# Selected and recent scores of the last attention as three products of rounded parts

## What is computed

```python
def nsa_attention(q, kc, vc, ks, vs, kw, vw, gate_logits, ...):
    qh = q.reshape(B_, S, NSA_KV, NSA_HPG, NSA_DH)... * (NSA_DH ** -0.5)
    ...
        sc = jnp.einsum('bghqd,bgjd->bghqj', qb, kcmp) + head_bias(rel_c)
        ...
        ss = jnp.einsum('bghqd,bgqkd->bghqk', qb, kg) + bias_s
        ps = masked_softmax(ss, (rel_s >= 0)[:, :, None])
        osel = jnp.einsum('bghqk,bgqkd->bghqd', ps, vg)
        ...
        sw = jnp.einsum('bghqd,bgkd->bghqk', qb, kwb) + head_bias(rel_w)
        pw = masked_softmax(sw, mask_w)
        ow = jnp.einsum('bghqk,bgkd->bghqd', pw, vwb)
        return gb[:, 0, ..., None] * oc + gb[:, 1, ..., None] * osel + gb[:, 2, ..., None] * ow
```

## Time and profile before

| | |
|---|---|
| median of 3 runs | 3185.5 us (3185.4 to 3188.45) |
| the profiled execution | 3188.14 us, its span 3186.6 us |
| busy: PE, PEld, DVE, ACT, POOL | 3063.3, 2472.8, 1313.5, 1186.2, 1105.1 us |
| granted TensorE clock, mean | 0.989 |
| the last attention, scores of the third unit to the end of the quarters | 2786.29 to 2996.00 us of the span |
| L1542 (all scores of this function) | 352 MATMUL records, 2177.7 to 2991.3 us |
| who waited for L1542 | DVE L1589, 119.1 us in 122 waits |

### The profile page before, as it was taken

The page is one execution under the profiler, slowest core; times in us unless marked ns, Lnnn a source line. Parts: engine busy times, 40 slices in busy tenths (PEclk is TensorE's granted clock), DMA queues, the critical chain, the costliest instruction groups (busy, mean ns, idle before and its releaser), DMA issues.

```text
span 3186.6 us, 36178 instructions
## 1 busy us (share of the span) xinstructions
PE 3063.3 (96%) x14292; PEld 2472.8 (78%) x14292; DVE 1313.5 (41%) x2362; ACT 1186.2 (37%) x2090; POOL 1105.1 (35%) x463
## 2 busy tenths in 40 slices
PE   8999998899999999999989999989999999999998
PEld 6888777678888878887858888877768878866787
DVE  5311386723111451112874231285544252256532
ACT  3222375743232442223424332353333342355432
POOL 4444432024444444444004444433424423300143
PEclk9999999999999999999999999999999999999999
DMA  4333232013333223333213333323313325400032
GB/s 146 93 99 97 83 123 69 1 47 99 99 93 99 93 86 99 98 95 100 89 40 113 99 99 93 99 89 104 100 53 99 93 89 179 132 2 1 28 98 73
DMA packets 78188, 278.27 MB, mean 87 GB/s; under 512 B 8600, under 2 KB 9496, under 8 KB 77637
## 3 DMA queue, kind: packets, MB, share of 16 engines
q1 hardware_dynamic: 78020, 275.96, 27.5%
HBM read 273.78 MB, written 6.08 MB: 88 GB/s over the span
## 4 chain that ended last, share of the span: by engine, by line
PE 84%; DVE 10%; ACT 3%; issue 2%; POOL 1%; DMA 0%; ACTq 0%; SPq 0%; DVEq 0%; POOLq 0%
PE ps L486 24%; PE ps L488 24%; PE ps L487 24%; PE ps L1568 3%; PE ps L1542 2%; DVE arena L2440 1%; DVE arena L1824 1%; PE ps L1554 1%; PE ps L3135 1%; PE ps L2490 1%; DVE w_lo L471 1%; PE ps L1988 1%; PE ps L2931 1%; PE ps L1974 1%; POOL w_lo L461 1%
## 5 line engine op out<-in xcount | busy, mean ns | idle before, releaser
L461 POOL TENSOR_TENSOR w_lo<-ring,w_hi 128x1024 fp32r<-128x1024 f32 x447 | 1090.5, 2441 | 1949.4 <-ACT w_hi L438 1908.0
L486 PE MATMUL ps<-x_hi,w_hi 128*128 128x512 f32 x2168 | 858.0, 396 | 35.0 <-POOL w_lo L461 21.9
L488 PE MATMUL ps<-x_hi,w_lo 128*128 128x512 f32 x2168 | 847.6, 391 | 0.0
L487 PE MATMUL ps<-x_lo,w_hi 128*128 128x512 f32 x2168 | 847.2, 391 | 0.0
L438 ACT CAST w_hi<-ring 128x1024 fp32r<-128x1024 f32 x473 | 493.9, 1046 | 723.9 <-PE ps L488 714.6
L486 PEld LDWEIGHTS ps<-x_hi,w_hi 128*128 128x128 f32 x2168 | 409.5, 189 | 127.9 <-issue 19.6
L487 PEld LDWEIGHTS ps<-x_lo,w_hi 128*128 128x128 f32 x2168 | 409.6, 189 | 88.2 <-issue 4.1
L488 PEld LDWEIGHTS ps<-x_hi,w_lo 128*128 128x128 f32 x2168 | 409.0, 189 | 86.2
L486 PE MATMUL ps<-r_hi,w_hi 128*128 128x512 f32 x1120 | 436.3, 390 | 0.0
L487 PE MATMUL ps<-r_lo,w_hi 128*128 128x512 f32 x1120 | 435.7, 389 | 0.0
L488 PE MATMUL ps<-r_hi,w_lo 128*128 128x512 f32 x1120 | 435.7, 389 | 0.0
(11 more groups left out here) (269 smaller groups left out, 3320.7 us busy)
## 6 DMA issues: line engine op xcount, KB each, us to landing
ring<-in_stream SPq DMA_DIRECT2D x473, 512.0 KB, 3.5
arena<-in_cmp_w SPq DMA_DIRECT2D x16, 512.0 KB, 3.8
frev_copies<-frev SPq DMA_DIRECT2D x16, 240.0 KB
arena<-frev_copies SPq DMA_DIRECT2D x1, 3072.0 KB, 13.1
h<-in_x SPq DMA_DIRECT2D x4, 512.0 KB, 8.0
out<-arena SPq DMA_DIRECT2D x4, 512.0 KB
arena<-in_p SPq DMA_DIRECT2D x2, 512.0 KB
arena<-in_mem SPq DMA_DIRECT2D x1, 1024.0 KB
```

The lines of the kernel that those rows point to most:

```text
L461: self.nc.gpsimd.tensor_tensor(self.w_lo[:, n % SPLIT, :], self.ring[:, n % RING, :], self.w_hi[:, n % SPLIT, :].bitcast(F32), ALU.subtrac ...
L486: nc.tensor.matmul(out, a[0], b[0], start=start, stop=False)
L487: nc.tensor.matmul(out, a[0], b[1], start=False, stop=False)
L488: return nc.tensor.matmul(out, a[1], b[0], start=False, stop=stop)
```

## The change

The scores of the selected and recent units (not of the compressed ones) are computed by `product` from high and low parts, of keys and of queries. The parts of the keys are made once in `compress_and_project`: ACT's evacuation of the last 4 groups writes float32r into `mem_hi`, and DVE, after its 64 small preparations, subtracts that from PSUM into `mem_lo` (4 of 128x512). The arrays of the memory operand serve as room for the keys' parts. The parts of a query are made in `attention`, once per group, two groups ahead: ACT rounds it to `r_hi` (`round`), DVE subtracts (`rest`) into `r_lo`; there are 8 places of 128 columns. ACT's rounding stands before the exponentials of a group's first unit, DVE's subtraction before the bias of a group's last unit. PE waits for the group's subtraction ahead of s and w. ACT also waits at the start for the values and for the keys' low parts.

```diff
-        self.w = key.shape[-1]
+        self.w = (key[0] if isinstance(key, tuple) else key).shape[-1]
+class Queries:
+    PLACES = 8
+    AHEAD = 2
+    def __init__(self, k, q, scored):
+        s = k.s
+        self.k, self.q, self.scored = k, q, scored
+        self.hi, self.lo = (x[:, :, :].rearrange("p a b -> p (a b)") for x in (k.r_hi, k.r_lo))
+        self.high, self.low = Reserved(s["query_high"], len(q)), Reserved(s["query_low"], len(q))
+    def place(self, g):
+        return slice(g % self.PLACES * P, (g % self.PLACES + 1) * P)
+    def parts(self, g):
+        return self.hi[:, self.place(g)], self.lo[:, self.place(g)]
+    def round(self, act, g):
+        if g >= len(self.q):
+            return
+        if g >= self.PLACES:
+            act.wait_ge(*self.scored(g - self.PLACES))
+        self.k.nc.scalar.copy(self.hi[:, self.place(g)], self.q[g]).then_inc(self.high.handle, 1)
+    def rest(self, dve, g):
+        if g >= len(self.q):
+            return
+        dve.wait_ge(self.high.handle, self.high.at(g + 1))
+        self.k.nc.vector.tensor_tensor(self.lo[:, self.place(g)], self.q[g], self.hi[:, self.place(g)].bitcast(F32),
+                                       ALU.subtract).then_inc(self.low.handle, 1)
...
-                nc.tensor.matmul(k.ps[:, i % 4, 0:u.w], u.q, u.key, start=True, stop=True).then_inc(scored.handle, 1)
+                if isinstance(u.key, tuple):
+                    g = int(group[i])
+                    pe.wait_ge(split.low.handle, split.low.at(g + 1))
+                    ins = k.product(k.ps[:, i % 4, 0:u.w], split.parts(g), u.key, True, True)
+                else:
+                    ins = nc.tensor.matmul(k.ps[:, i % 4, 0:u.w], u.q, u.key, start=True, stop=True)
+                ins.then_inc(scored.handle, 1)
...
+            if split:
+                for g in range(split.AHEAD):
+                    split.rest(dve, g)
             for i in range(n + 5):
+                if split and i < n and units[i].last:
+                    split.rest(dve, int(group[i]) + split.AHEAD)
...
+            if split:
+                for token in after:
+                    act.wait_ge(*token)
+                for g in range(split.AHEAD):
+                    split.round(act, g)
             for i in range(n + 3):
+                if split and i < n and units[i].first:
+                    split.round(act, int(group[i]) + split.AHEAD)
...
+            for m in range(4):
+                u = NSA_H + m
+                dve.wait_ge(read.handle, read.at(u + 1))
+                hi, lo = (x[:, m * SEQ:(m + 1) * SEQ] for x in keys)
+                nc.vector.tensor_tensor(lo, k.ps[:, 4 + u % 4, :], hi.bitcast(F32), ALU.subtract).then_inc(lows.handle, 1)
...
-        k.bank_read[4 + b] = read.token(n - 3 + b)
+        k.bank_read[4 + b] = lows.token(b + 1)
...
-    keys = k.at(scr + ATTENTION + 2048 + NSA_H * BIASW, 4, SEQ)
+    keys = [x[:, :, :].rearrange("p a b -> p (a b)") for x in (k.mem_hi, k.mem_lo)]
...
-                         else nc.scalar.copy(keys[:, m - NSA_H, :], ps), compressed[-1], second_loaded)
+                         else nc.scalar.copy(keys[0][:, (m - NSA_H) * SEQ:(m - NSA_H + 1) * SEQ], ps), keys,
+                         compressed[-1], second_loaded)
...
-    attention(k, units, scr, after=values[-1:])
+    attention(k, units, scr, after=values[-1:] + [keys_ready], queries=True)
```

More of the change, by code:

```diff
@@ L350, in __init__ @@
                  "proj_part", "proj_read", "rope_swapped", "rope_added", "roped", "factor_ready", "lifted", "lift_copied", "sub_squared", "sub_summed",
-                 "sub_rooted", "sub_inverted", "sub_spread", "sub_made", "sub_applied")
+                 "query_high", "query_low", "keys_low", "sub_rooted", "sub_inverted", "sub_spread", "sub_made", "sub_applied")
         self.s = {n: Signal(ctx.enter_context(nc.semaphore(n))) for n in names}
@@ L1510, in __init__, with attention @@
         self.first, self.last, self.dst, self.clamp, self.steps = first, last, dst, clamp, steps
-        self.w = key.shape[-1]
-def attention(k, units, scratch, background=(), after=(), in_place=True):
+        self.w = (key[0] if isinstance(key, tuple) else key).shape[-1]
[23 more added lines that the diff above has]
+                                       ALU.subtract).then_inc(self.low.handle, 1)
+def attention(k, units, scratch, background=(), after=(), in_place=True, queries=False):
     nc, s = k.nc, k.s
@@ L1531, in attention @@
     last_of = {int(group[i]): i for i in range(n)}
+    split = Queries(k, [u.q for u in units if u.first], lambda g: scored.token(last_of[g] + 1)) if queries else None
     with Stage(nc) as block:
@@ L3066, in second_even, with compress_and_project @@
     return sums
-def compress_and_project(k, kc, vc, kcmp, vcmp, scr, w1, evacuate, after, second_loaded):
+def compress_and_project(k, kc, vc, kcmp, vcmp, scr, w1, evacuate, keys, after, second_loaded):
     nc, s = k.nc, k.s
@@ L3078, in compress_and_project @@
     ready, part, hidden, second = s["dve_step"], s["pe_step"], s["act_step"], s["pe_step2"]
-    done, read, copied = s["product_done"], s["evacuated"], s["cmp_copied"]
+    done, read, copied, lows = s["product_done"], s["evacuated"], s["cmp_copied"], s["keys_low"]
     first, n = STREAM_AT["nsaqk"]
@@ L3182, in compress_and_project @@
     for b in range(4):
-        k.bank_read[4 + b] = read.token(n - 3 + b)
+        k.bank_read[4 + b] = lows.token(b + 1)
     copied.advance(3)
+    lows.advance(4)
     for g, v in ((ready, n), (part, n), (hidden, 4), (second, 3), (done, n), (read, n)):
@@ L3211, in second_odd @@
                          lambda m, ps: nc.scalar.mul(y[:, m, :], ps, -(P ** -0.5)) if m < NSA_H
-                         else nc.scalar.copy(keys[:, m - NSA_H, :], ps), compressed[-1], second_loaded)
+                         else nc.scalar.copy(keys[0][:, (m - NSA_H) * SEQ:(m - NSA_H + 1) * SEQ], ps), keys,
+                         compressed[-1], second_loaded)
+    keys_ready = s["keys_low"].token()
     def evac(j, t, ps):
@@ L3243, in second_odd @@
             for b in range(2):
-                units.append(Unit(qh, keys[:, 2 * b + g, 0:w], bias[:, h, SEQ - w:SEQ],
+                at = (2 * b + g) * SEQ
+                units.append(Unit(qh, tuple(x[:, at:at + w] for x in keys), bias[:, h, SEQ - w:SEQ],
                                   [(P, vals[:, j, b * 256 + g * P:b * 256 + (g + 1) * P]) for j in range(i + 1)],
```

## The result

| | before | after |
|---|---|---|
| median | 3186.07 us (19 runs, 3184.95 to 3188.89) | 3192.64 us (19 runs, 3191.56 to 3197.77) |
| the profiled execution | 3188.14 us | 3191.63 us, its span 3190.3 us |
| granted TensorE clock, mean | 0.989 | 0.984 |

The ratio of the times is 1.0024, with a 95% interval of 1.0017 to 1.0030: slower, by some 7.6 us (5.4 to 9.6). The forecast, 3187.1, said no change that a measurement can tell (under 6.4 us). The result lies inside its range of 3182.5 to 3194.5, but 5.5 us above its number and past those 6.4 us. The runs of after lie in two heaps: thirteen at 3191.6 to 3194.3, six at 3197.0 to 3197.8. The profiled execution is one of the first heap, near its lower end.

The account below looks back on a forecast made before the run. It took a loop through PE, DVE and ACT to bound each group of the last attention. Terms -3.1, -1.2, +1.0, +3.9 and +1.0 summed to +1.6 us on 3185.5, giving 3187.1 us, range 3182.5 to 3194.5.

Parts of the forecast that it names:

- narrow products at full price: Rival, last quarter: a 128-column product costs 0.22 us like a whole float32 matmul, +0.44 a score; 3193.8 us; chance 0.22.
- i = 3: First quarter of the last attention, 512-column scores, twelve groups: -0.26 us a group, -3.1 us in all.
- i = 2: Second quarter of the last attention, 384-column scores, twelve groups: -0.10 us a group, -1.2 us in all.
- i = 1: Third quarter of the last attention, 256-column scores, twelve groups: +0.08 us a group, +1.0 us in all.
- i = 0, instructions: Last quarter, 128-column scores: +0.10 us in all twelve groups and +0.27 in ten, +3.9 us in all.
- start: Start of the last attention: two subtractions come first and the first long score waits for one; +1.0 us, bounds +0.3 and +1.4.
- Scores on PE: Three products replace one float32 matmul: -0.18, -0.14 and -0.08 us a long score at 512, 384 and 256 columns.
- The subtraction: DVE's query subtraction between store and bias of w, 46 times: 0.27 us each, less DVE's room of 0.35, 0.23, 0.11, none.
- The floor for narrow products: Last quarter: weight loads set the pace of 128-column products, 0.106 us each, 0.32 for three, +0.10 a score.
- The rival of quick weight loads: Rival, last quarter: weight loads beat the floor, three narrow products take 0.19 us; sum 0, 3185.5 us; chance 0.09.
- The turn between kinds: Rival: the first product after float32 work pays 0.1 us more, 48 times in s; +4.8, 3191.9 us; chance 0.05.
- The hidden subtraction: Rival: DVE's subtraction costs nothing, so w gains as s does; -6.5 us in all, 3179.0 us; chance 0.06.

Follow-up runs that it names:

- experiment four: The changed kernel with DVE's query subtraction moved ahead of the bias of s instead of the bias of w; 3195.95 us, ratio to before 1.0032.
- experiment two: The changed kernel with the last quarter's products 256 columns wide instead of 128, the extra columns unused; 3185.82 us, ratio to before 0.9996.
- experiment three: The changed kernel with all scores in float32 and keys as before; queries still rounded and subtracted, the parts unread; 3190.12 us, ratio to before 1.0025.
- experiment one: The changed kernel with the last quarter's 128-column scores in float32 and no query parts there; 3182.46 us, ratio to before 0.9987.

## Why the prediction's range held and its mechanism did not

That 3192.64 lies within the stated range is luck. The range reached up to 3194.5 to take in narrow products at full price, which did not happen, and what filled it was a fall of the clock that the prediction did not have. The change is also past the 6.4 us that the prediction set as the least to be told from none, an outcome to which it gave 0.22, most of it for that same full price.

The step that failed is its frame: "the granted clock is 1.00 throughout", read off before and then taken for the changed kernel as well. The sum had no term for the clock and no rival had one. Term by term:

| term (us) | forecast | measured | what was off |
|---|---|---|---|
| i = 3 | -3.1 | -3.78 | subtraction 0.27, was 0.13 |
| i = 2 | -1.2 | -2.74 | the same |
| i = 1 | +1.0 | -0.67 | the same |
| i = 0, instructions | +3.9 | +2.3 (12 x 0.19) | subtraction; a narrow score +0.10, was +0.06 for s |
| i = 0 and tail, clock | none | +9.7 | missing |
| start | +1.0 | +2.64 | half clock in it, 1.3 |

The fifth row is +10.95 + 1.08 less twelve groups at 2.91 - 2.72 = 0.19. Without it the stage would have come out at some -2.3 us: the change's own work saves a little, and the clock takes it back four times over. (A slip in the forecast's fourth row: in the two groups without a subtraction w grows by 0.10 too, +0.2 in all.)

- **Scores on PE:** right for the long ones. Three products of 512 columns save 0.16 us a score where 0.18 was read, those of 256 save the 0.08 that was read (experiment four, where the subtraction is out of the way), and the idle time before the bias of w went.
- **The subtraction:** the mechanism was right, the size was not. I took off one overlap with a neighbour and there are two. With 0.13 the sum's rule (the change of s, plus the later of two ways) gives -0.36, -0.24 and -0.06 a group; measured are -0.32, -0.23 and -0.06, and +0.06 + 0.13 = 0.19 in the last quarter, where groups went from 2.72 to 2.91. The Trainium skill, "VectorE: DVE Perf Modes", section "The TRN2 errata", gives (N+151)/0.96 ns for a float32 add of two tensors; 0.29 us at 128 columns is an estimate from it, and the trace agrees on the instruction's length (0.281). That is a length and not a cost: here the net cost was less than half of it. The prediction set this 0.29 against its 0.27, from which one overlap had already been taken, and so had the sum 0.8 us higher by it; less the same overlap it is 0.21, and the sum some 2.8 us lower.
- **The floor for narrow products:** right within 0.01 (0.11 to 0.12 from start to start after the first, the floor 0.106); the scores of s and w grew by 0.06 and 0.09 where the floor said 0.10 each. The Trainium skill, "TensorE: Matmul & The Clock Gate", section "LDWEIGHTS (loading the stationary operand)", gives columns over 1.2 in ns for a weight load, from which 107 ns for 128 is an estimate; the trace agrees with it in the distance of the starts. The rival of quick weight loads, 0.063 a product, is refuted: the rows show no starts closer than 0.11.
- **Full price for narrow products:** refuted by the rows at full clock above and by experiment two. Its time, 3193.8, was near the result by accident.
- **The turn between kinds:** seen, and not paid. The timeline of PE in after at i = 3, the scores of s:

```profile
2826.97 0.48 PE L486 MATMUL ps<-mem_hi,r_hi 128*128 128x512 f32 x1
2827.29 0.39 PE L487 MATMUL ps<-mem_lo,r_hi 128*128 128x512 f32 x1
2827.52 0.39 PE L488 MATMUL ps<-mem_hi,r_lo 128*128 128x512 f32 x1
```

  The first product takes 0.32 to the next start and the second 0.23. But the group at i = 3 shrank by 0.32 where the rule gives 0.36, so of the rival's 0.1 a group at most 0.04 is left, and nothing at i = 2 and 1.
- **The hidden subtraction:** half true, and worth what the first three quarters gained over the forecast.
- **The signs of being wrong altogether:** PE waiting in the loop and ACT's roundings in the way were not seen. The third, a stage that begins more than 1.5 us later, came true with 2.64, and half of that is the clock.

What the runs show of the clock's cause is this much. Float32 scores and no parts in the last quarter: no fall there (before, and five kernels). Narrow products with or without the subtraction: a fall in every profile (after and three kernels), and a mean clock below before's in every run of these. Products of 256 columns: none in the profile. Subtraction and rounding alone: some runs with, some without. Busy time did not announce it: PE was busy for 11.25 of 11.89 us ahead of the fall in after, and for 31.41 of 32.30 in the same quarter and 65.50 of 72.36 in the first, where before kept its clock. ACT's rounding by itself was not tried, and neither was a delay of the same length without work. Why short products and a busier DVE turn the balance was not measured, and I have no number for it.

## What to carry to other kernels

A full granted clock in the trace of before need not hold after an edit, even one that leaves PE's instructions alone. Where an edit makes matmuls shorter and more numerous in a stage of small dependent steps, give the fall of the clock a rival, with a price from rows at the lower level (here each group of 2.91 us took 1.27 more). Convert only the widths that gain: three float32r products for one float32 matmul saved 0.16, 0.12 and 0.08 us a score at 512, 384 and 256 columns, and lost 0.06 to 0.09 at 128. Leaving the narrow quarter alone turned +0.24% into -0.13%, and the first group float32 as well made it -0.22% to -0.27%.

## What the runs showed of the hardware

- The granted clock fell to the 1.2 GHz level inside a running stage, with PE busy for 11.25 of the 11.89 us before, and did not come back for 34 us (after), past the end of the stage, although PE was busy without a gap (26.96 of 26.96 us).
- At half clock narrow products start 0.21 us apart, 0.11 to 0.12 at full clock. A 512-column product starts 0.43 us after its neighbour at half clock, 0.227 at full.
- Whether it falls can differ from run to run of one kernel: by times and mean clocks seven runs without and five with, 12 us apart (experiment three). How long it stays down can too: 3.4 us in one profile and 13.7 in another behind the same instructions (after and experiment one, at the start).
- Wider products with more columns to compute made the kernel 6.8 us faster than narrow ones, although at full clock their groups took longer (2.99 us against 2.91): the clock held (experiment two).
- An edit of DVE's and ACT's work only was enough to change TensorE's clock (experiment three).
- A 128-column subtraction of 0.281 us, put between two other DVE instructions, cost 0.13 us net, as it overlaps both by 0.08.
